# One hybrid layer with experts: head rows spread by broadcast transfers instead of matmuls, inputs in four pieces, and another order around the first expert pair

## What is computed

```python
def token_mixers(x, w_in, ...):
    proj = x @ w_in                      # split into the inputs of all branches
    xa = causal_conv(lru_x, lru_conv_w) + lru_conv_b
    ha = rg_lru(xa, ...) * gelu(lru_y)
    hb = mlstm_chunkwise(ml_q, ml_k, ml_v, ml_i + ml_i_bias, ml_f + ml_f_bias)
    qkv = silu(causal_conv([gd_q, gd_k, gd_v], gd_conv_w)); q, k = l2_norm(q), l2_norm(k)
    g = -exp(gd_a_log) * softplus(gd_a + gd_dt_bias); beta = sigmoid(gd_b)
    hc = gated_delta_chunked(q, k, v, g, beta)
    merged = sigmoid(gate_0) * (ha @ w_br_lru) + sigmoid(gate_1) * (hb' @ w_br_ml) + sigmoid(gate_2) * (hc' @ w_br_gd)
    return merged @ w_out

def gated_delta_chunked(q, k, v, g, beta):       # chunks of 64 tokens, 8 heads
    gc = cumsum(g)
    gam = exp(where(causal, gc[:, None] - gc[None, :], -inf))
    a_mat = where(strict, beta[:, None] * gam * (k @ k.T), 0)
    sol = triangular_solve(eye + a_mat, [beta * v, beta * exp(gc) * k])
    ...

def reference(...):
    x = layer_norm(ALPHA * x + token_mixers(x, ...), ln1_g, ln1_b)
    x = layer_norm(ALPHA * x + moe_ffn(x, ...), ln2_g, ln2_b)

def moe_ffn(x, ...):
    gate, e = softmax(top_k(x @ router_w + router_b, 4))
    hdn = x[tok] @ w1[e] + b1[e]; glu = min(hdn[:, :1024], 7); lin = clip(hdn[:, 1024:], -7, 7)
    y = (glu * sigmoid(1.702 * glu) * (lin + 1)) @ w2[e] + b2[e]     # summed with its gate into the token's row
```

## Time and profile before

| | |
|---|---|
| median of 3 runs | 1371.64 us (1370.78 to 1375.32) |
| profiled execution, its own time | 1371.29 us |
| its span | 1369.5 us |
| granted TensorE clock, mean | 0.998 |
| TensorE matmul busy | 1297.3 us (95%) |
| VectorE busy | 338.6 us (25%) |
| ScalarE busy | 159.9 us (12%) |
| moved by DMA | 460.71 MB, mean 336 GB/s |
| chain that ended last | TensorE 69%, DMA 28%, VectorE 3% |

### The profile page before, as it was taken

One profiled execution on the slowest core, in us unless ns is written; L12 is line 12 of the kernel. 1 busy time (PEld: TensorE's weight loads), 2 busy tenths in 40 slices (PEclk: granted clock), 3 DMA queues, 4 the chain that ended last, 5 costly groups with the idle time before them and its releaser, 6 DMA issues.

```text
span 1369.5 us, 17664 instructions
## 1 busy us (share of the span) xinstructions
PE 1297.3 (95%) x7512; PEld 716.2 (52%) x7512; DVE 338.6 (25%) x739; ACT 159.9 (12%) x263; POOL 9.7 (1%) x17
## 2 busy tenths in 40 slices
PE   7999999999989999999999989899998989989895
PEld 6888888888877443444434434343343433434341
DVE  3847573122135112012011020111201011020113
ACT  1441612011001100000000000000000000000001
POOL 0010000000000000000000000000000000000000
PEclk9999999999999999999999999999999999999999
DMA  6432322324896899999999999999999999999994
GB/s 237 154 123 97 112 93 93 125 106 139 308 384 246 349 427 425 427 427 427 429 428 429 428 429 428 428 429 428 427 429 429 429 428 428 429 428 429 428 429 188
DMA packets 44774, 460.71 MB, mean 336 GB/s; under 512 B 11169, under 2 KB 11809, under 8 KB 14657
## 3 DMA queue, kind: packets, MB, share of 16 engines
q1 hardware_dynamic: 38176, 455.23, 80.0%
q10 hardware_dynamic: 6560, 4.94, 1.1%
HBM read 458.71 MB, written 1.44 MB: 336 GB/s over the span
## 4 chain that ended last, share of the span: by engine, by line
PE 69%; DMA 28%; DVE 3%; issue 0%; SPq 0%; ACT 0%; DVEq 0%
PE ps L849 21%; PE ps L487 19%; DMA mix<-expert_w 14%; DMA ring<-expert_w 12%; PE ps L867 8%; PE ps L807 4%; PE ps L795 4%; PE ps L505 3%; PE ps L842 3%; PE ps L728 2%; PE ps L497 1%; DMA mix<-stream_w 1%; PE ps L858 1%; DMA mix<-x_turned 1%; DMA ring<-small_w 1%; PE ps L914 1%
## 5 line engine op out<-in xcount | busy, mean ns | idle before, releaser
L849 PE MATMUL ps<-ring,mix 128*64 128x512 f32 x1536 | 343.3, 592 | 0.0
L487 PE MATMUL ps<-mix 128*128 128x256 f32 x1248 | 273.7, 380 | 2.2 <-DVE ring L1488 2.2
L487 PEld LDWEIGHTS ps<-mix 128*128 128x128 f32 x1248 | 235.9, 190 | 35.7 <-issue 4.1
L849 PEld LDWEIGHTS ps<-ring,mix 128*64 128x64 f32 x1536 | 108.6, 137 | 196.1 <-issue 190.7
L867 PE MATMUL ps<-ring,mix 128*64 128x512 f32 x768 | 175.6, 596 | 31.0 <-DMA ring<-expert_w 31.0
L1780 DVE TENSOR_SCALAR mix<-ps 128x512 f32<-128x512 f32 x32 | 22.1, 692 | 516.9 <-PE ps L849 516.9
L867 PEld LDWEIGHTS ps<-ring,mix 128*64 128x64 f32 x768 | 55.1, 137 | 138.3 <-issue 105.6
L849 PE MATMUL ps<-mix 128*64 128x512 f32 x512 | 115.4, 592 | 0.0
L1789 DVE COPY mix<-ps 128x512 f32<-128x512 f32 x32 | 22.1, 692 | 244.3 <-PE ps L858 244.3
L849 PEld LDWEIGHTS ps<-mix 128*64 128x64 f32 x512 | 36.2, 137 | 68.7 <-issue 66.5
L867 PE MATMUL ps<-mix 128*64 128x512 f32 x256 | 58.2, 596 | 13.5 <-DMA mix<-expert_w 13.5
(11 more groups left out here) (260 smaller groups left out, 768.5 us busy)
## 6 DMA issues: line engine op xcount, KB each, us to landing
ring<-expert_w SPq DMA_DIRECT2D x144, 2048.0 KB, 33.0
mix<-expert_w SPq DMA_DIRECT2D x48, 2048.0 KB, 32.0
mix<-stream_w SPq DMA_DIRECT2D x42, 1024.0 KB, 4.8
mix<-stream_w SPq DMA_DIRECT2D x10, 512.0 KB, 4.4
mix<-x_turned SPq DMA_DIRECT2D x2, 512.0 KB, 6.0
mix<-planes ACTq DMA_DIRECT2D x1, 1024.0 KB, 9.6
mix<-ln_g ACTq DMA_DIRECT2D x2, 512.0 KB, 8.2
mix<-ln_b ACTq DMA_DIRECT2D x2, 512.0 KB, 9.7
```

Source lines behind the costliest of these rows:

```text
L487: ins = mm(o[:, m * S:(m + 1) * S], w[:, c, m * P:(m + 1) * P], rhs[:, c, :], start=(m == 0 and c == 0), stop=(c == nk - 1), skip_group_ch ...
L849: ins = mm(PS[64 * a:64 * a + 64, bank + g, :], XE[j][:, c, 64 * a:64 * a + 64], w[:, a * D + g * 512:a * D + g * 512 + 512], start=False, ...
```

## The change

Four edits go together. **Head rows**: bb, gb, gr and mr are gone from TensorE and from the banks. SP writes the rows to three small HBM buffers behind the load of lx0 and reads them back with a broadcast over partitions, straight into `EG`, `GAM` and `ME` behind lx1 and into `KB` behind ly0; ScalarE and VectorE then work in place. **First inputs**: x and the first weights come in four pieces each, x from ScalarE's queue and the weights from SP's; `first_proj` runs over the row blocks in its outer loop; `small_w` follows x without a wait, and the next two weight items wait for the pieces. **First pair**: TensorE gathers half of the second block, does two chunks, gathers the rest, does the other six of `up(0, ...)`, and `gT`, residuals and scatter come later (the gates in a buffer of their own, `GT0`). **Steps**: step 3 is no longer loaded behind wo0 but behind the rows of x, and step 9, the first into place 0 again, comes as two halves, each behind one used chunk. Its core:

```diff
-FILL = (("mq", "mk", "mr0", "mr1", "lg"), ("ms00", "ms10", "ms01", "ms11", "mv0"), ("mv1",), ("mo0", "mn"),
+FILL = (("mq", "mk", "lg"), ("ms00", "ms10", "ms01", "ms11", "mv0"), ("mv1",), ("mo0", "mn"),
...
-    order += [("bb0", 4), ("bb1", 5), ("gb0", 6), ("gb1", 7)]
...
-    order += [(f"gr{n}", 4 + n) for n in range(4)]
...
+        rows_gb = nc.dram_tensor("rows_gb", (2, GH, S), F32, kind="Internal").ap()
+        rows_gt = nc.dram_tensor("rows_gt", (NT, GH, P), F32, kind="Internal").ap()
+        rows_m = nc.dram_tensor("rows_m", (MH, 3, P), F32, kind="Internal").ap()
...
-            early = [stream_at[name] for name in ("br20", "br21", "br22", "wo0")]
-            half = KD // 2 * GW
-            for h in range(2):
-                sp.dma_start(XT[:, 4 * h:4 * h + 4, :], x_turned[:, 4 * h:4 * h + 4, :]).then_inc(E(f"x_in{h}"), 16)
-                sp.dma_start(WB[0].rearrange("p c n -> p (c n)")[:, h * half:(h + 1) * half],
-                             stream_w[0, :, h * half:(h + 1) * half]).then_inc(E("w_in0" if h else "first_in"), 16)
+            early = [stream_at[name] for name in ("br20", "br21", "br22")]
+            for k in range(QUARTERS):
+                first, last = KD // QUARTERS * k, KD // QUARTERS * (k + 1)
+                sp.dma_start(WB[0].rearrange("p c n -> p (c n)")[:, first * GW:last * GW],
+                             stream_w[0, :, first * GW:last * GW]
+                             ).then_inc(E("w_in0" if k == QUARTERS - 1 else f"first_in{k}"), 16)
             for n, (name, src, col) in enumerate(stream):
                 if n == 0:
                     continue
                 buf, loaded = WB[n % WBUFS], E(f"w_in{n % WBUFS}")
+                if n == 1:
+                    sp.wait_ge(E("first_in2"), 32)
+                if n == 2:
+                    sp.wait_ge(E("wsm_in"), 16)
...
+                if name == "lx0":
+                    sp.wait_ge(E("rows_ready"), 1)
+                    sp.wait_ge(E("rows_ready_act"), 3)
+                    sp.dma_start(rows_gb[0], RW[64:64 + GH]).then_inc(E("rows_out"), 16)
+                    sp.dma_start(rows_gb[1], RW[96:96 + GH]).then_inc(E("rows_out"), 16)
+                    sp.dma_start(rows_gt.rearrange("t h l -> h t l"), RW[64:64 + GH].rearrange("h (t l) -> h t l", t=NT)
+                                 ).then_inc(E("rows_out"), 16)
+                    sp.dma_start(rows_m[:, 0:2, :], NM[0:MH].rearrange("h (b l) -> h b l", b=2)
+                                 ).then_inc(E("rows_out"), 16)
+                    sp.dma_start(rows_m[:, 2, :], NM[0:MH, P:2 * P]).then_inc(E("rows_out"), 16)
+                if name == "lx1":
+                    sp.wait_ge(E("rows_out"), 80)
+                    for a in range(2):
+                        sp.dma_start(EG[64 * a:64 * a + 64], rows_gb[0].rearrange("(j a) s -> a j s", a=2)[a]
+                                     .partition_broadcast(64)).then_inc(E("eg_in"), 16)
+                    sp.dma_start(GAM, rows_gt.rearrange("t h l -> (t h l)").rearrange("(n q) -> n q", n=4)
+                                 .partition_broadcast(P)).then_inc(E("gam_in"), 16)
+                    sp.dma_start(ME, rows_m.partition_broadcast(P)).then_inc(E("me_in"), 16)
+                if name == "ly0":
+                    sp.wait_ge(E("gsilu"), 1)
+                    for a in range(2):
+                        sp.dma_start(KB[64 * a:64 * a + 64, :, a, :], rows_gb[1].rearrange("(j a) s -> a j s", a=2)[a]
+                                     .partition_broadcast(64)).then_inc(E("beta_in"), 16)
...
+            for n in range(STEPS):
+                sp.wait_ge(E("chunk_used"), n + 1)
+                sp.dma_start(PLACES[0][:, 2 * D * n:2 * D * (n + 1)],
+                             expert_w[0, FIRST + 2, :, 2 * D * n:2 * D * (n + 1)]).then_inc(E("steps_in0"), 16)
...
-            load_turn(0, 0, FIRST + 2)
+            load_turn(0, 0, FIRST + 3)
...
-                for m in range(2):
-                    for c in range(KD):
-                        if m == 0 and c % 4 == 0:
-                            pe.wait_ge(E(f"x_in{c // 4}"), 16)
-                            pe.wait_ge(E("w_in0" if c else "first_in"), 16)
+                for c in range(KD):
+                    k, new = divmod(c, KD // QUARTERS)
+                    if new == 0:
+                        pe.wait_ge(E(f"first_in{k}"), 32 if k < QUARTERS - 1 else 16)
+                        if k == QUARTERS - 1:
+                            pe.wait_ge(E("w_in0"), 16)
+                    for m in range(2):
                         ins = mm(o[:, m * S:(m + 1) * S], WB[0][:, c, m * P:(m + 1) * P], XT[:, c, :],
...
-            for n in range(2):
-                o = take(f"bb{n}")
-                for m in range(2):
-                    for a in range(2):
-                        ins = mm(o[64 * a:64 * a + 64, m * S:m * S + S],
-                                 ident[:, 96 + 4 * n + 2 * m + a:97 + 4 * n + 2 * m + a].to_broadcast([P, 64]),
-                                 RW, start=True, stop=True, skip_group_check=True)
-                done(f"bb{n}", ins)
...
-            for n in range(4):
-                many(f"gr{n}", [(m * S, m * S + S, ident[:, 64 + 2 * n + m:65 + 2 * n + m].to_broadcast([P, P]), RW)
-                                for m in range(2)])
...
-                    elif name[:2] == "mr":
...
+                        again = place == 0 and (not isinstance(turn, int) or m > FIRST + 1)
+                        pe.wait_ge(E(f"steps_in{place}"), 16 * (PB * EC // STEPS // SLOTS) * turn
+                                   + 16 * ((m - 1) // SLOTS) + (32 if again else 16))
...
-                    gather(1, 2, (1,))
-                    count_all()
-                    for c in range(4):
-                        pe.wait_ge(E("xe_first" if c < 3 else "xe_ready"), c % 3 + 1)
+                    gather(1, 2, (1,), (0, 1))
+                    for c in range(KD):
+                        if c == 2:
+                            gather(1, 2, (1,), (2, 3))
+                            count_all()
+                        pe.wait_ge(E("xe_first" if c % 4 < 3 else "xe_ready"), c - c // 4 + 1 if c % 4 < 3 else c // 4 + 1)
                         up(0, c, one)
-                    pe.wait_ge(E("gates_ready"), 1)
-                    o = take("gT")
-                    for t in range(NT):
-                        ins = mm(o[0:NE, t * P:(t + 1) * P], GAT[:, t, 0:NE], ident, start=True, stop=True,
-                                 skip_group_check=True)
-                    done("gT", ins)
-                    pe.wait_ge(E("x1_ready"), 2)
-                    for t in range(NT):
-                        for h in range(2):
-                            residual(t, h)
-                    pe.wait_ge(E("ys_ready"), 1)
-                    scatter(None)
...
+                if first:
+                    pe.wait_ge(E("x1_ready"), 2)
                 gather(0, two + 1)
-                up(0, 4, one)
+                if not first:
+                    up(0, 4, one)
                 pe.wait_ge(E("gt_ready"), i + 1)
                 gather(1, two)
-                for c in range(5, KD):
-                    up(0, c, one)
+                if first:
+                    pe.wait_ge(E("gates_ready"), 1)
+                    o = take("gT")
+                    for t in range(NT):
+                        ins = mm(o[0:NE, t * P:(t + 1) * P], GAT[:, t, 0:NE], ident, start=True, stop=True,
+                                 skip_group_check=True)
+                    done("gT", ins)
+                else:
+                    for c in range(5, KD):
+                        up(0, c, one)
 
                 pe.wait_ge(E("xe_ready"), 2 * i + 4)
                 bias(1, two)
                 for c in range(6):
                     up(1, c, two)
+                    if first and c in (1, 3):
+                        for h in range(2):
+                            residual(c // 2, h)
+                if first:
+                    pe.wait_ge(E("ys_ready"), 1)
+                    scatter(None, GT0)
...
+            for k in range(QUARTERS):
+                first, last = KD // QUARTERS * k, KD // QUARTERS * (k + 1)
+                act.dma_start(XT[:, first:last, :], x_turned[:, first:last, :]).then_inc(E(f"first_in{k}"), 16)
+            act.dma_start(WSM, small_w).then_inc(E("wsm_in"), 16)
             act.dma_start(VC, vectors).then_inc(E("vec_in"), 16)
             act.dma_start(SC[:, 32:34], row_bias).then_inc(E("bias_in"), 16)
-            act.wait_ge(E("x_in1"), 16)
-            act.dma_start(WSM, small_w).then_inc(E("wsm_in"), 16)
+            act.wait_ge(E(f"first_in{QUARTERS - 1}"), 16)
...
-                full(act, f"gb{n}")
-                A(EG[:, 2 * n:2 * n + 2, :], ps(f"gb{n}").rearrange("p (c s) -> p c s", s=S), ACT.Exp
-                  ).then_inc(free(f"gb{n}"), 1)
+                act.wait_ge(E("eg_in"), 32)
```

(13 more changed lines are left out.)

79 lines of the change are left out of this document (22 added, 57 removed).

## The result

| | before | after |
|---|---|---|
| median | 1371.74 us (4 runs) | 1355.98 us (1355.27 to 1356.90, 4 runs) |
| ratio | | 0.9878, 95% interval 0.9866 to 0.9890 |
| profiled execution, its span | 1369.5 us | 1353.9 us |
| matmul busy | 1297.3 us | 1288.1 us |
| moved by DMA | 460.71 MB | 463.62 MB |

The change makes the kernel 1.22% faster; 1357.0 (1.07%) was forecast. The spans differ by 15.6 us, the sum on record was 14.6.

A forecast was written before the change was run, and what follows sets the result against it. The prediction took the expert weight queue, 180 steps at 4.909 us, to fix the end. Savings of 2.2 + 8.2 + 3.7 + 0.5 = 14.6 us gave 1356.7, forecast as 1357.0 us, range 1353.5 to 1362.0.

The forecast's parts named there:

- the sum on record: Whole kernel: savings of 2.2, 8.2, 3.7 and 0.5 us, together 14.6 us.
- What bounds the kernel: Expert part: the weight queue fixes the end at 4.909 us per step; TensorE time saved ahead counts fully.
- The start: 2.2 forecast: Kernel start: inputs in four pieces let the first matmul begin 2.2 us sooner; bounds 0 and 3.4.
- the rival that it spoke for: Kernel start: first pieces land at full rate, TensorE starts 1.2 us earlier, time 1355.8; chance 0.07.
- Head rows: 8.2 forecast: Before and around the solve: dropping 28 row-spreading matmuls saves 3.6 + 4.1 + 0.5 us; bounds 0 and 9.4.
- The rival of idle row groups: At the solve: VectorE and ScalarE set the pace, so row groups give nothing; price 8.2 us, chance 0.06.
- Step 3 behind x: 3.7 forecast: Output projection: without step 3 ahead, the stalls for wo1 and wo2 go, 3.7 us; bounds 0 and 3.7.
- First pair: +0.5 forecast: First expert pair: reordering saves 0.5 us, bounds -0.5 and 1.5; step 9's halves worth nothing.
- the second look of the bound's part: Expert queue: step 22 found it 1.5 us deep, so an earlier stream gains at most 1.5 us, starting at step 22.
- the hole: Weight queue's idle stretch at 455 to 460 us, at 3 GB/s, expected to close with the first pair's reordering.
- Waits for wo2, wo3 or x: Output projection: queues share, so wo2 is late or x holds VectorE; price 3.7 us, chance 0.09.
- Another rate of the stream: Expert part: the 180 steps run at another rate, 1.8 us per 0.01; chance 0.03 slower, 0.02 within 0.3%.

The follow-up runs named there:

- both refills eased: Changed kernel with pair 0's scatter behind the second down group and, in later pairs, the sixth up group ahead of the second gather: 1356.93 us, ratio 0.9886.
- scatter moved: Changed kernel with pair 0's scatter of the bias rows behind the second group of down products: 1356.63 us, ratio 0.9878.
- gelu moved too: Changed kernel with pair 0's scatter later, the sixth up group before later pairs' second gather, and VectorE's gelu behind the mLSTM scores: 1353.45 us, ratio 0.9868.

## Why the forecast came out, point by point

**What bounds the kernel.** Shown. The steps take 4.911 us each (forecast 4.91), and every microsecond that TensorE won ahead of the experts came out at the end: 15.66 at the output projection's third group, 15.63 at the last wait. The other runs show it too. Ten traces have no wait for weights and no stretch of half clock behind the start of the output projection. That start lies anywhere from 375.64 to 382.50 us in them, and from there to the last wait all ten take 956.6 to 957.4.

**The start: 2.2 forecast, 3.0 measured.** In this pair of traces the first quarter landed sooner than the 5.2 us that I took: the first matmul began at 4.85, 2.56 us earlier. The rest is mostly the pace of the first 32 products, 9.31 us from the first of them to small's against 9.66, with 0.08 us of waiting for small_w in the latter. The 3.0 is good to no better than about 1 us: in the second trace of the kernel before, the first matmul began at 6.76 and small's products at 16.46, and in the eleven traces that load in quarters small's begin anywhere from 13.48 to 14.79. Against the mean of those, 14.2, the two traces before give 2.3 and 2.9, so 2.2 was at the low end and not clearly mis-sized. I had read the 17.07 of the earlier trace rows as the time small_w landed. With the old start TensorE waited for it 0.08, 0.93 and 0.44 us in the three traces, so its early issue has a worth that I put at nothing. No piece was waited for. By the Trainium skill, "DMA: Bandwidth & Descriptors", section "Anatomy of one DMA", the quarter was to land near 3.9 us by the estimate. The page gives its fit for transfers that GpSimd issues, and these come from SyncE and ScalarE. The trace lies between that estimate and mine, nearer to mine, and the rival that it spoke for (1.2 us earlier still) did not come. That the median, 1355.98, is nearer to this rival's 1355.8 than to my 1357.0 is chance: the missing microsecond came from four terms and not from the first pieces.

**Head rows: 8.2 forecast, 8.5 measured.** bb, gb and gr gave 10.92 - 3.0 = 7.9 (forecast 7.7), mr gave 0.6 (0.5), and the wait of 1.18 us that takes the rest was forecast at 1.2, in its place. VectorE never waited for beta or the decay rows: SP issues beta's reads at 66.5, khat begins at 73.08 and the work behind it follows without a wait. The gamma instructions took 4.29 us from SBUF, as good as the 4.23 before. The rival of idle row groups fell; of the 10.2 us that undoing them cost ahead of the output projection, 8.5 are theirs.

**Step 3 behind x: 3.7 forecast, 4.1 measured.** No wait is left in the output projection. But undoing this edit alone gives back only 2.2 us of TensorE's time, and 1.7 to 1.9 at the last wait. The remaining 1.9 (1.5 by the second trace of the kernel before) goes with the state of the rest: in both traces of the kernel before, step 3 took 10.7 us to land and TensorE waited 3.5 to 3.7, with step 3 put back into the changed kernel it took 9.4. The difference lies behind the landing of wo0: step 3 landed 6.3 us behind it in both traces before, and 4.9 in the run. What sped up that one transfer is not settled: no run tells it, and the issue times around it are the same. So 2.2 us are shown to be this edit's, the rest is only known to go with the whole.

**First pair: +0.5 forecast, 0.0 measured.** The step that failed is the second look of the bound's part. I reasoned that the hole would close and step 22 become the start of the unbroken stream. The hole moved to 464 to 468 instead, since step 15 waits for the 14th chunk used but step 16 for the 18th, and the scatter that the change puts in front of it (3.6 us) stands there. TensorE's own cost was put too low, at 0.5 to 0.6 us for two short waits: by the start of pair 1, at 478.50, the lead is down to 14.75 from 15.66, so it is 0.9, and the queue gives that back. The old order ran within 0.3 us, and the halves made no difference, as the forecast said of them. The kernel before takes from the output projection to the last wait 961.24 and 964.22 us in its two traces. Less its stalls for wo1 and wo2 (4.1 and 3.7), and two stretches of half clock in the second, that is 957.1 in both, which is what the changed kernel takes.

**The other rivals.** Waits for wo2, wo3 or x: none came. Another rate of the stream: none. The sum was 1.0 us short, and less than its parts suggest, since the first pair's miss of 0.5 has the other sign.

## What to carry to other kernels

Where a queue at its rate sets the end, count a saving ahead of it fully, and behind its start by the next refill that comes too late: freeing one late refill only hands the bound to the next, so list them all before pricing one. Price a removed group of instructions by the wait that its neighbour then shows, not by its busy time: mr had 1.7 us and gave 0.6. When an edit is undone alone and gives back less than it took, look at what the rest of the change did to the same transfer before crediting the edit.

## What the runs showed of the hardware

**A clock that drops to half for a short stretch, in some executions.** The spans of five experiments hold 1.7 us that their edit does not explain, one of them twice. These are windows of the same stretch, first of the changed kernel, then of the one with mr by matmul (10 us, then 2 of it); the third number from the end is TensorE's granted clock:

```profile
190.00:200.00 10.00, 7.83 (x37) 6.94 (x37) 8.98 (x30) 6.25 (x21) 0.00 (x0) 1.00 0.01 2
```

```profile
190.00:200.00 10.00, 7.83 (x33) 6.58 (x33) 8.64 (x30) 5.18 (x20) 0.00 (x0) 0.83 0.01 2
...
195.00:197.00 2.00, 2.00 (x6) 1.55 (x6) 1.72 (x10) 1.98 (x8) 0.00 (x0) 0.50 0.00 0
```

TensorE waits 2.17 us in both (L1500, L1505), and behind it the same 64 products took 14.05 us in the one and 15.74 in the other. In the second the clock stood at 0.50, the 1.2 GHz level, from 1.2 us behind the first product on. In the other traces it fell between just ahead of that product and 1.2 us behind it, and each stretch cost 1.7 us. It fell there in the runs with the inputs in halves, the rows by matmul, mr by matmul, the old pair order and step 9 whole, and in the second trace of the kernel before, so in 6 of 14 traces. The others, the first trace of the kernel before and both of the changed kernel among them, show none. The kernel before has it in one trace and not in the other, so the edit is not what decides. The second trace of the kernel before showed it at two more places. One is behind its wait for wo1 (5.41 us instead of 3.72 for 16 products, above). The other, at 426.03, has no wait in front of it, and neither has the second one of the run with the rows by matmul, at 419.06. There TensorE had been at short products of 128 and 32 columns, in the same part of both kernels. So a wait is not needed. These are the six products at that place, after the change and with the rows by matmul:

```profile
408.19 1.54 PE L741 MATMUL ps<-mix 128*128 128x256 f32 x6
```

```profile
418.96 2.82 PE L741 MATMUL ps<-mix 128*128 128x256 f32 x6
```

The 12 runs of the kernel before reach from 1370.48 us at a mean clock of 0.998 to 1375.33 at 0.994. The changed kernel, having no wait for weights, may have fewer places where it can lose 1.7 us. That is argued, from one trace; but on the second chip it stood at 1355.96 against a median of 1373.13, 17.2 us apart where the first chip had 15.8. The Trainium skill, "TensorE: Matmul & The Clock Gate", section "The HAM clock gate", says that the clock is halved or full by how busy the engine has been, and that the number of matmuls at half clock at a kernel's start varies between executions. These rows agree with the two levels, and show such a variation far behind the start too.

**When a step lands behind the one ahead of it.** In the unbroken stream 2 MB land 4.9 us apart. Step 22 did so when it was issued with 4.0 us of transfers ahead of it (both refills eased) and with 3.5 (after), and did not with 2.2 (7.1 us behind step 21, scatter moved). Step 16 with 1.9 and 1.7 ahead landed 7.2 and 6.9 behind its own (scatter moved, both refills eased). But the depth of the queue does not decide alone. Steps 17, 20 and 23 after the change landed 5.8, 5.8 and 5.6 us behind theirs with 3.4, 7.0 and 4.9 us ahead; with the gelu moved too, step 23 landed 7.0 behind with 3.6 ahead; and in the second trace of the changed kernel it landed 4.9 behind with 5.4. So there is a second cause, which no run here isolates and which differs between traces of one kernel. From an empty queue a step took 7.5 to 8.0 us from its issue.
